# Round 0 of the experts: feature columns by one-hot matmuls on the rows kept on chip, instead of a gather from DRAM and eight turns

## The reference, cut to what matters

```python
scores = jax.nn.sigmoid((hf @ w_router).astype(jnp.float32))
...
expert = group[:, None] * EXPERTS_PER_GROUP + local      # two of 16, both in one group
...
xb = hf[buf_tok].reshape(n_blocks, MOE_BLOCK, d)         # rows of tokens, sorted by expert

def expert_block(args):
    xblk, e = args
    return (jax.nn.silu(xblk @ w_gate[e]) * (xblk @ w_up[e])) @ w_down[e]
```

## Time and profile before

| | |
|---|---|
| median of 3 runs | 1646.56 us (1641.74 to 1651.41) |
| profiled execution | 1646.47 us |
| its span | 1644.7 us |
| TensorE (PE) busy | 1428.9 us, 87% |
| VectorE (DVE) busy | 675.1 us, 41% |
| ScalarE (ACT) busy | 306.5 us, 19% |
| POOL busy | 74.0 us, 4% |
| mean DMA rate | 204 GB/s |

### The profile page before, as it was taken

The page is one execution under the profiler, slowest core; times in us unless marked ns, Lnnn a source line. Parts: engine busy times, 40 slices in busy tenths (PEclk is TensorE's granted clock), DMA queues, the critical chain, the costliest instruction groups (busy, mean ns, idle before and its releaser), DMA issues.

```text
span 1644.7 us, 22361 instructions
## 1 busy us (share of the span) xinstructions
PE 1428.9 (87%) x9741; PEld 734.0 (45%) x9741; DVE 675.1 (41%) x1046; ACT 306.5 (19%) x500; POOL 74.0 (4%) x201
## 2 busy tenths in 40 slices
PE   5999999967888795899999959969998769999992
PEld 3445565526766443433333344535654433333331
DVE  2114334236677316323333235785643543332334
ACT  2221211133232103000000042221112300000002
POOL 7000000000000000000000010000000000000001
PEclk9999999978899897899999979989999879999996
DMA  9685674030001007899997761201100699999884
GB/s 345 212 306 183 201 253 131 1 141 15 3 2 46 10 0 297 351 426 376 351 426 290 293 244 52 74 29 51 52 0 0 248 359 393 385 333 425 337 345 166
DMA packets 91502, 335.21 MB, mean 204 GB/s; under 512 B 6552, under 2 KB 37516, under 8 KB 75020
## 3 DMA queue, kind: packets, MB, share of 16 engines
q1 hardware_dynamic: 76880, 287.94, 45.8%
q10 hardware_dynamic: 8476, 23.82, 3.7%
q0 software_dynamic: 6048, 22.02, 3.5%
HBM read 310.70 MB, written 23.07 MB: 203 GB/s over the span
## 4 chain that ended last, share of the span: by engine, by line
PE 73%; DVE 13%; DMA 7%; ACT 5%; issue 2%; POOL 0%; ACTq 0%; SPq 0%; DVEq 0%; POOLq 0%
PE banks L1731 19%; PE banks L1285 14%; PE banks L1753 10%; PE banks L1657 5%; DVE work L1867 4%; PE banks L1326 4%; PE banks L1274 4%; PE banks L1221 3%; DMA work<-in_w_down_dram 2%; PE banks L1714 2%; PE banks L1641 2%; DMA ring<-in_w_ada_dram 1%; DMA h_rows<-y_features 1%; DVE work L1873 1%; DMA work<-h_rows,idx_tok 1%
## 5 line engine op out<-in xcount | busy, mean ns | idle before, releaser
L1285 PE MATMUL banks<-h_features,ring 128*128 128x512 f32 (+1 forms) x656 | 293.5, 602 | 5.6 <-ACT h_features L899 4.0
L1731 PE MATMUL banks<-ring,work 128*64 128x512 f32 x672 | 233.0, 611 | 2.3 <-issue 2.3
L1731 PE MATMUL banks<-work 128*64 128x512 f32 x512 | 212.2, 595 | 0.0
L1285 PEld LDWEIGHTS banks<-h_features,ring 128*128 128x128 f32 (+1 forms) x656 | 122.3, 190 | 159.7 <-issue 156.4
L1867 DVE TENSOR_TENSOR work<-work,banks 128x256 f32<-128x256 f32 (+2 forms) x88 | 47.7, 565 | 193.5 <-PE banks L1731 146.0
L1753 PE MATMUL banks<-work 128*64 128x512 f32 x320 | 112.7, 593 | 0.0
L1867 DVE TENSOR_TENSOR work<-work 128x512 f32<-128x512 f32 (+9 forms) x202 | 100.2, 496 | 14.5 <-ACT work L1094 3.6
L1731 PEld LDWEIGHTS banks<-ring,work 128*64 128x64 f32 x672 | 72.4, 140 | 72.8 <-issue 67.3
L1753 PE MATMUL banks<-ring,work 128*64 128x512 f32 x256 | 98.4, 592 | 0.0
L1657 PE MATMUL banks<-y_features,ring 128*128 128x512 f32 x192 | 84.7, 603 | 6.4 <-DVE small L2399 6.4
L1731 PE MATMUL banks<-h_features,work 128*64 128x512 f32 x192 | 86.3, 595 | 2.2 <-ACT work L1144 2.2
(11 more groups left out here) (361 smaller groups left out, 1806.4 us busy)
## 6 DMA issues: line engine op xcount, KB each, us to landing
ring<-in_w_up_dram SPq DMA_DIRECT2D x16, 2048.0 KB, 12.9
y_features<-in_w_ada_dram SPq DMA_DIRECT2D x28, 1024.0 KB, 5.7
work<-in_w_down_dram SPq DMA_DIRECT2D x14, 2048.0 KB, 13.8
ring<-in_w_gate_dram SPq DMA_DIRECT2D x12, 2048.0 KB, 9.4
work<-in_w_up_dram SPq DMA_DIRECT2D x10, 2048.0 KB, 13.9
work<-in_w_gate_dram SPq DMA_DIRECT2D x10, 2048.0 KB, 12.7
ring<-in_w_ada_dram SPq DMA_DIRECT2D x8, 2048.0 KB, 12.1
h_features<-in_w_gate_dram SPq DMA_DIRECT2D x8, 2048.0 KB, 8.7
```

The lines of the kernel that those rows point to most:

```text
L1285: ins = mm(PS[0:w, b, :], lhsT=W[:, k, c0:c0 + w], rhs=h[:, k, :], start=(k == 0), stop=(k == KD - 1))
L1731: ins = mm(PS[rows, bank, :], lhsT=xt[:, k, rows], rhs=ws[lane][:, k, :], start=(k == 0), stop=(k == KD - 1))
```

## The change

The rows are kept in `y_features` by blocks of features: ScalarE's copy out of PSUM reads every eighth element, so that block k of a row holds the features 8q+k. The DRAM copy gets the same order, and `turn_x` reads 128 contiguous elements.

Round 0's columns are no longer gathered and turned. TensorE multiplies, for each of the eight blocks of features, the four tiles of rows in `y_features` with the one-hot matrix `ohf` and adds them up in PSUM (`first_x`); the result has the place and the form that the eight turns gave. The matmuls that found the row numbers, the cast and its two signals go. POOL's first gather is the one for round 1. The semaphore of the turns is now raised by `first_x` for round 0. SP no longer waits for the first gather; ahead of the load into `y_features` it waits for `first_x`.

```diff
@@ SP: loads of the weights
                     if earlier is None and home == 7:
                         sp.wait_ge(sem(f"l{l}_rows_stored"), 16 * NT)
+                        sp.wait_ge(sem(f"l{l}_xt_turned"), 1)
...
                                 sp.wait_ge(sem("table_ready"), l + 1)
-                                sp.wait_ge(gathered[l][0], 16)
@@ POOL: gathers
-                pool.wait_ge(sem("first_rows_known"), l + 1)
+                pool.wait_ge(sem("rows_known"), l + 1)
...
-                for r in range(ROUNDS + 1):
-                    if r == 1:
-                        pool.wait_ge(sem("rows_known"), l + 1)
+                for r in range(1, ROUNDS + 1):
@@ ScalarE: rows out of PSUM
-                    act.activation(y_[:, t * D:(t + 1) * D], PS[:, b:b + 2, :].rearrange("p a b -> p (a b)"), ACT.Copy)\
-                       .then_inc(sem("rows_copied"), 1)
+                    act.activation(y_[:, t * D:(t + 1) * D].rearrange("p (k q) -> p k q", k=KD),
+                                   PS[:, b:b + 2, :].rearrange("p a b -> p (a b)").rearrange("p (q k) -> p k q", k=KD),
+                                   ACT.Copy).then_inc(sem("rows_copied"), 1)
@@ TensorE
-                pe.wait_ge(sem("choices_ready"), 3 * l + 2)
-                for t in range(NT):
-                    ins = mm(PS[:, 7, 0:1], lhsT=ohf[:, 2 * t:2 * t + 2, :].rearrange("p a b -> p (a b)"),
-                             rhs=tokid[:, t:t + 1], start=(t == 0), stop=(t == NT - 1))
-                ins.then_inc(sem("rank_ready"), 1)
+
+                def first_x():
+
+                    pe.wait_ge(sem("choices_ready"), 3 * l + 2)
+                    pe.wait_ge(sem("rows_copied"), NT * (l + 1))
+                    for k in range(KD):
+                        for t in range(NT):
+                            ins = mm(PS[:, 2 + k // 4, (k % 4) * P:(k % 4 + 1) * P], lhsT=y_[:, t * D + k * P:t * D + (k + 1) * P],
+                                     rhs=ohf[:, 2 * t:2 * t + 2, :].rearrange("p a b -> p (a b)"),
+                                     start=(t == 0), stop=(t == NT - 1))
+                    ins.then_inc(sem(f"l{l}_xt_turned"), 1)
...
-                        ins = tr(PS[:, 2 + k // 4, (k % 4) * P:(k % 4 + 1) * P], xg[:, j, k:D:8], ident)
+                        ins = tr(PS[:, 2 + k // 4, (k % 4) * P:(k % 4 + 1) * P], xg[:, j, k * P:(k + 1) * P], ident)
...
-                turn_x(0, 16)
+                first_x()
@@ VectorE
-                dve.wait_ge(sem("rank_ready"), 3 * l + 2)
-                signal(dve.tensor_copy(idx_tok[:, 0:1], PS[:, 7, 0:1]), "first_rows_known")
```

More of the change, by code:

```diff
@@ L1772, in experts @@
                         lanes_down(r - 1, weights(2, r - 1), r - 1 if r > 1 else None)
-                        turn_x((r + 1) % 2, 16 * ((r + 1) // 2 + 1))
+                        turn_x((r + 1) % 2, 16 * (r // 2 + 1))
                     lanes_up(1, weights(1, r), xTb[r % 2], range(KD)).then_inc(sem(f"l{l}_up_done"), 1)
@@ L1794, in experts @@
                     lanes_up(1, again(1), xTb[ROUNDS % 2], range(KD)).then_inc(sem(f"l{l}_up_done"), 1)
-                    turn_x((ROUNDS + 1) % 2, (it + ((ROUNDS + 1) // 2 + 1)) * 16)
+                    turn_x((ROUNDS + 1) % 2, (it + (ROUNDS // 2 + 1)) * 16)
                     turn_act(it + ROUNDS)
@@ L2461, in choose @@
                 link(tt(gk, gk, bc(gsum, 2, 1), ALU.mult))
-                dve.wait_ge(sem("rank_ready"), 3 * l + 1)
+                dve.wait_ge(sem("rank_ready"), 2 * l + 1)
                 link(tt(rank, PS[:, 4, 0:NT * E].rearrange("p (a b) -> p a b", b=E), both, ALU.subtract))
@@ L2531, in choose @@
                 link(dve.tensor_copy(idx_dest[:, :], f2(destf)))
-                dve.wait_ge(sem("rank_ready"), 3 * l + 3)
+                dve.wait_ge(sem("rank_ready"), 2 * l + 2)
                 signal(dve.tensor_copy(idx_tok[:, 1:MAX_BLOCKS], PS[:, 6, 1:MAX_BLOCKS]), "rows_known")
```

## The result

| | median us | runs | ratio to before (95% interval) |
|---|---|---|---|
| before, first group | 1650.56 | 13 | |
| changed kernel | 1638.83 (1631.18 to 1649.12) | 13 | 0.9938 (0.9919 to 0.9957) |
| before, second group | 1649.28 | 24 | |
| changed kernel, second group | 1641.80 (1633.63 to 1646.40) | 12 | 0.9964 (0.9941 to 0.9987) |

What follows compares the result with a forecast made beforehand. Behind round 0 the expert stage was taken as bound by TensorE. A gain of 18.3 us less 1.4 for gather waits, 16.9, took 1646.47 to 1629.6 us; range 1625 to 1636, with rivals 2 and 3 1623 to 1640.

Steps and rivals of the forecast that it cites:

- rival 3: Round 1's gather comes as late as the slowest one, 4.3 us in each layer: 1636.8 us; chance 0.12.
- Bound: Expert stage behind round 0 is bound by TensorE, so an earlier start of round 0 moves everything behind it.
- The step: Round 0's 64 new matmul instructions, partly at half clock: 10.5 us in layer 0, 9.9 in layer 1.
- Rivals 1 and 2: Round 0's new step: clock never comes back, 1643.6 us, chance 0.12; clock back at once, 1624.6 us, chance 0.09.
- transposes don't count for the clock: Turns ahead of round 0's gate did nothing for the clock; otherwise the new step about 1.5 us longer per layer.
- What is late next: Round 1's gather takes 9.8 us, so TensorE waits 0.95 us in layer 0, 0.5 in layer 1; sum 1.4.
- rule of taking turns between queues: Alternative for round 1's gather beside weight loads: lands at some 5.3 us, without a wait; sum 1627.8 us.
- The base: Round 0's first 20 gate instructions, nearly all at half clock before, gain 2.7 and 2.0 us at full clock.
- Strided copies: ScalarE's copies out of PSUM stay at 1.02 us; up to 2.2 us each would be hidden. Slower-kernel rival: chance 0.03.
- weights of round 1: Gate weights load goes out at about 662 and is there by 672; round 1 begins at about 675.
- SP's new wait: Load overwriting the rows waits for the new matmuls, which end at 657 (662.3 at half clock), no later than its turn.
- third signal: VectorE's signal before the tokens_of_blocks group, at 658.77; TensorE arrives at 662.8, so the wait stays covered by 4 us.

Runs made afterwards that it cites:

- filler run: Changed kernel plus three f32 matmuls of 512 columns, result unread, where TensorE waits for round 1's gather; ratio to before 0.9913 (0.9884 to 0.9943).

## Why the prediction missed

The sign was right, and so was what the change takes off the path. The size was wrong: 16.9 us forecast, 10.2 and 5.9 measured; by A to B it is 8.1 us (means 84.0 to 75.9). Two steps failed: the gather of round 1 was sized too short, and the half clock that its wait brings was not in the sum. That the median of 1638.83 lies within the wide range of 1623 to 1640, and near rival 3's 1636.8, is in part luck: that rival has a longer wait than was measured and no half clock. Point by point:

- **Bound.** Right. From B to the end of the stage's last down projection it is 253.6 to 254.7 us in 23 of the 24 stages traced and 255.7 in one, so the gain is kept.
- **The step.** 10.5 and 9.9 us forecast, 9.04, 9.86, 8.93 and 9.15 measured. The half clock at its start was there, in layer 0 for 3.4 us instead of 5.2 (in layer 1 until 5.2 us behind the start instead of 4.4, the second time 3.7), and an instruction at full clock takes 0.112 and not 0.12. That gave 1.9 us more in sum than forecast. Rivals 1 and 2 (no clock, full clock at once) did not happen. The reading of the Trainium skill, that transposes don't count for the clock (TensorE: Matmul & The Clock Gate, Part 4: PE-mode transpose), stays open: no run here has turns alone for long enough.
- **The gather of round 1.** This is the step that failed, the term "What is late next". Its wait was taken as 0.95 and 0.5 us, from the row in which a gather ran beside two weight loads (9.8 us). It was 2.92 and 3.05, then 3.63 and 3.17, with 11.2 to 11.9 us from issue to landing. The sum is short by 5.0 us. In layer 0 of the first trace 2.0 us are missing. Of these 1.4 are the gather's length, 11.2 for 9.8: the first gather of the kernel before had two loads beside it and no more, this one had two and 2.2 us later a third, with a second gather between. The other 0.6 is its issue, 2.94 us behind the group of tokens_of_blocks instead of 2.35. VectorE's cast came as soon as before, but POOL took 1.05 us from it to the issue, where it had taken 0.46 before (674.31 to 674.77):

```profile
674.31 0.18 DVE L2533 CAST idx_tok<-banks 128x19 int32<-128x19 f32 x1 [12.57 <-PE banks L1707]
```

Why POOL takes longer here is open. That the gather might be late was named, and rival 3 (4.3 us a layer, chance 0.12) lies nearer to the 3.2 us measured on the mean than the forecast's 0.7 does. The Trainium skill's rule of taking turns between queues (DMA: Bandwidth & Descriptors, Queues, rings and completion order) led to an estimate of 5.3 us; no trace bears that out, since one weight load beside it already makes 6.7 to 8.9. (Without a wait the prediction's own terms give 1628.2 there and not 1627.8.)

- **What the wait does to the clock.** Missing altogether. A wait of 3 us on TensorE was counted as 3 us; with it came 1.5 to 2.9 us of gate at half clock, and once 0.88 at the turns, 4.3 us in sum. The filler run shows the wait and its half clock apart. The text had the pieces: it had read a half clock behind idle time at the gate of round 0 and did not ask the same of the idle time that it forecast.
- **The base.** The 2.7 and 2.0 us for a gate at full clock were read from the slower of two traces. In the second trace of before the gate begins earlier and A to B is 3.7 us less in sum, 1.8 on the mean of two.
- **Strided copies, weights of round 1, SP's new wait, third signal.** Right: the copies take 1.02 us, and TensorE has no wait for these weights or for the third signal in the changed kernel's traces.

The sum: 16.9, less 5.0 for the gather, less 4.3 for the clock behind it, less 1.8 for the base, plus 2.4 for the step, the gate and the turns (1.9, 0.4 and 0.1), is 8.2 against the 8.1 of the traces.

## What to carry to other kernels

When a wait for a transfer is taken off the path, list the next transfer that the same engine will wait for, and when it will be issued against the bulk loads: loads that hang on another event stay where they are and now run beside it. Delaying bulk loads that aren't needed soon can be worth more than the change itself; here one wait on SP, which put off one load and the two queued behind it, more than doubled the gain (19.3 us from A to B instead of 8.1). Price a wait on TensorE with the half clock behind it: the seven waits of 2.7 to 4.4 us ahead of round 1 in these traces all had one, the five of 0.2 to 0.7 us, two of them behind filler, had none. And forecast a stage of 40 us from two traces, not one.

## What was not expected of the hardware

The clock can fall well after the idle time. In layer 0 of the changed kernel TensorE stood still from about 668.9 to 671.8, ran eight turns at full clock and stood still for the copy, and only at about 674.2 was the clock at 0.5, for about 3.5 us, with TensorE busy. In layer 1 it fell during the wait and stayed low for about 6.8 us, so waits of about the same length cost more or less (1.5 to 2.9 us at the gate, and in this layer 0.88 us at the turns).

A gather of 512 KB beside loads of 2 MB is slowed well out of proportion to its bytes: 4.0 to 4.6 us alone, 6.7 to 8.9 beside home 6's load, 9.2 to 9.8 beside two loads issued with it (the first gather of the kernels that have one), 11.2 to 12.7 beside two with a third behind. As an estimate, its 0.5 MB at the 400 to 450 GB/s of the windows would account for about 1.2 us.
